# Which side of a trip through HBM is cut into 1 KB rows: the turned blocks of a hybrid SSM and attention encoder layer

## What is computed

```python
h = rms_norm(x, g_mix)
proj = h @ w_in                       # z | xBC | dt_fwd | dt_bwd | q | k | v | gate_ssm | gate_attn
y_ssm = mamba2_bidir(z, xbc, dt_f, dt_b, ...)
y_attn = gqa_bidir_blocks(apply_rope(rms(q)), apply_rope(rms(k)), v)
merged = sigmoid(gate_a) * (y_ssm @ w_ssm_up) + sigmoid(gate_b) * (y_attn @ w_attn_up)
x = x + merged @ w_out
h2 = rms_norm(x, g_mlp)
x = x + square(relu(h2 @ w_mlp_in)) @ w_mlp_out
out = rms_norm(x, g_final)
```

## The kernel before

| rounds | put | get (waits for the put, `s_put`) | first use of what was got (waits `s_got`) |
|---|---|---|---|
| z gate, 4 | p = 6 | p = 1 of the next window | p = 5 |
| rope, 5 | p = 7 | p = 2 of the next window | p = 5 |
| merged, 3, and residual, 3 | p = 1 | p = 3 of the same window | p = 6 |

## Time and profile before

### The profile page before, as it was taken

One profiled execution on the slowest core, in us unless ns is written; L12 is line 12 of the kernel. 1 busy time (PEld: TensorE's weight loads), 2 busy tenths in 40 slices (PEclk: granted clock), 3 DMA queues, 4 the chain that ended last, 5 costly groups with the idle time before them and its releaser, 6 DMA issues.

```text
span 1607.3 us, 20614 instructions
## 1 busy us (share of the span) xinstructions
PE 1595.4 (99%) x7984; PEld 1349.2 (84%) x7984; DVE 1278.8 (80%) x1521; ACT 928.0 (58%) x1264; POOL 79.2 (5%) x67
## 2 busy tenths in 40 slices
PE   9999999999999999999999999999999999999998
PEld 7888888888888888888888888888888888888886
DVE  7978877888767688876666667999899988998893
ACT  7665566665666545554445555665566655655562
POOL 3000000000000134000000000000000000000000
PEclk9999999999999999999999999999999999999999
DMA  7665656665688776545877875558645863686461
GB/s 272 202 201 184 201 183 211 197 198 185 196 244 238 231 225 200 172 145 181 244 265 235 278 228 178 181 171 266 188 133 200 275 192 123 204 281 214 143 244 53
DMA packets 144993, 327.93 MB, mean 204 GB/s; under 512 B 10944, under 2 KB 19328, under 8 KB 144768
## 3 DMA queue, kind: packets, MB, share of 16 engines
q1 hardware_dynamic: 129376, 302.21, 58.5%
q10 hardware_dynamic: 15520, 24.41, 5.2%
HBM read 316.55 MB, written 10.03 MB: 203 GB/s over the span
## 4 chain that ended last, share of the span: by engine, by line
PE 95%; DVE 2%; issue 1%; DMA 1%; ACT 0%; POOL 0%; POOLq 0%; SPq 0%; ACTq 0%
PE G L1835 17%; PE G L1836 17%; PE G L1837 17%; PE G L1844 13%; PE S L1844 7%; PE G L1848 6%; PE S L1835 4%; PE S L1836 4%; PE S L1837 4%; PE S L1848 4%; PE S L1962 1%; DMA raw<-in_w_in 1%; DVE wlo L1108 1%; PE S L1990 0%; PE S L1939 0%
## 5 line engine op out<-in xcount | busy, mean ns | idle before, releaser
L668 ACT ACTIVATE whi<-raw 128x1024 fp32r<-128x1024 f32 x395 | 416.6, 1059 | 396.4 <-PE G L1837 230.4
L1108 DVE TENSOR_TENSOR wlo<-raw,whi 128x1024 fp32r<-128x1024 f32 x395 | 483.3, 1238 | 132.1 <-ACT whi L668 130.5
L1835 PE MATMUL G<-whi,a_both 128*128 128x512 f32 x768 | 300.0, 391 | 2.5 <-DVE wlo L1108 2.0
L1837 PE MATMUL G<-whi,a_both 128*128 128x512 f32 x768 | 299.0, 389 | 0.0
L1836 PE MATMUL G<-wlo,a_both 128*128 128x512 f32 x768 | 299.0, 389 | 0.0
L1844 PE MATMUL G<-a_both,whi 128*128 128x512 f32 x640 | 201.5, 396 | 0.0
L1835 PEld LDWEIGHTS G<-whi,a_both 128*128 128x128 f32 x768 | 144.2, 188 | 34.0 <-issue 2.8
L1837 PEld LDWEIGHTS G<-whi,a_both 128*128 128x128 f32 x768 | 144.2, 188 | 30.2
L1836 PEld LDWEIGHTS G<-wlo,a_both 128*128 128x128 f32 x768 | 144.2, 188 | 28.9
L1848 PEld LDWEIGHTS G<-a_both,wlo 128*128 128x128 f32 x640 | 120.2, 188 | 28.3
L1835 PE MATMUL G<-whi,b_hi 128*128 128x512 f32 x342 | 133.5, 390 | 0.0
(11 more groups left out here) (313 smaller groups left out, 2689.1 us busy)
## 6 DMA issues: line engine op xcount, KB each, us to landing
raw<-in_w_in SPq DMA_DIRECT2D x208, 512.0 KB, 4.4
raw<-in_w_mlp_in SPq DMA_DIRECT2D x74, 512.0 KB, 4.6
raw<-in_w_mlp_out SPq DMA_DIRECT2D x74, 512.0 KB, 4.9
gates<-in_w_mlp_in SPq DMA_DIRECT2D x54, 512.0 KB, 4.2
gates<-in_w_mlp_out SPq DMA_DIRECT2D x54, 512.0 KB, 4.8
raw<-in_w_ssm_up SPq DMA_DIRECT2D x32, 512.0 KB, 3.8
raw<-in_w_attn_up SPq DMA_DIRECT2D x32, 512.0 KB, 4.5
raw<-in_w_out SPq DMA_DIRECT2D x32, 512.0 KB, 5.2
```

The costliest lines, as they stand in the source:

```text
L668: act.activation(high(m), piece(n), ACT.Copy).then_inc(hi_made, 1)
L1108: dve.tensor_tensor(low(m), piece(n), high(m).bitcast(F32), ALU.subtract).then_inc(lo_made, 1)
L1835: pe.matmul(out_ap, hi[:, k, cols], w_hi, start=start, stop=False)
L1837: return pe.matmul(out_ap, lo[:, k, cols], w_hi, start=False, stop=stop)
```

## The change

`put_blocks` issues four transfers instead of one, one for each j. Each takes 128 partitions by 256 floats and writes them as 4 by 32 rows of 1024 bytes, so that the exchange of i and j happens on the way out. `get_blocks` then brings 128 rows of 4096 bytes back with one transfer instead of four. The counts that others wait for follow: `s_put` rises by 64 a round instead of 16, `s_got` by 16 instead of 64. The diff:

```diff
@@ put_blocks
             act.wait_ge(blocks_turned, d + 1)
-            act.dma_start(block_rows[d], src.rearrange("p j c b t -> p (j c b t)")).then_inc(s_put, 16)
+            rows = block_rows[d].rearrange("(j w) (i x) -> j i w x", j=4, i=4)
+            for j in range(4):
+                act.dma_start(rows[j], src[:, j, :, :, :].rearrange("p c b t -> p (c b t)")).then_inc(s_put, 16)
@@ get_blocks
-            act.wait_ge(s_put, 16 * (d + 1))
+            act.wait_ge(s_put, 64 * (d + 1))
             if d:
                 act.wait_ge(lined, d)
-            rows = block_rows[d].rearrange("(i w) (j x) -> j w i x", i=4, j=4)
-            for j in range(4):
-                act.dma_start(dst[Q * j:Q * (j + 1), :, :, :, :].rearrange("w i c b t -> w i (c b t)"), rows[j]
-                              ).then_inc(s_got, 16)
+            act.dma_start(dst[:, :, :, :, :].rearrange("p i c b t -> p (i c b t)"), block_rows[d]).then_inc(s_got, 16)
@@ split_high, and the same in heads_in
-                act.wait_ge(s_got, 64 * (d + 1))
+                act.wait_ge(s_got, 16 * (d + 1))
@@ turn_blocks
-                dve.wait_ge(s_put, 16 * d)
+                dve.wait_ge(s_put, 64 * d)
```

## The result

The changed kernel takes **1641.4 us** (median of 4 runs, 1640.64 to 1644.03) against 1609.44 of the kernel before on the same chip: ratio 1.0197, 95% interval 1.0184 to 1.021. It is 31.7 us slower. The forecast was 1613.4 with a range up to 1626; the sign was right, and the size was eight times too small. The profiled execution took 1640.87 us.

The account below looks back on a forecast made before the run. PE was taken to bound the kernel, busy 99% of the span, so the change could only cost: 1609.39 + 3.5 (third merged round) + 0.5 (five ordinary rounds) = 1613.4 us, range 1608.5 to 1626.

Parts of the forecast that it names:

- the cover of 5.84 us: Steady state of ACT's weight conversions: one may start 5.84 us late before PE runs dry.
- the deadline: Longest time a put may take from issue before PE loses: 12.5 us in the first merged round.
- Four engines: Each put's destination has outermost size 4, so only four DMA engines carry it, 128 rows each; taken with 0.85.
- Two to three of them fall in until ACT stops: 2.5 to 3.7 us: Ordinary merged and residual rounds: weight pieces sharing the put's engines, 1.23 us each, put landing after 10.9 to 12.1 us.
- the prediction's own signs: Main step wrong if small packets stay at 10944; price wrong if PE has gaps in the first two merged rounds.
- My upper bound: Weights alternate packet for packet until four pieces are through: an ordinary put needs 15.1 us, kernel 1626.
- the row with both queues waiting: Profile row: 363 and 362 packets in 3 us, one of each in 132 ns, so engines alternate fairly.
- 0.5 us for all five: Five ordinary merged and residual rounds: ACT stands still some 7 us, PE loses nothing; 0.5 us allowed in all.
- rival 2: All six tight rounds overrun at the wait on `s_put`; 1622 at a put of 14.5 us; chance 0.18.
- The third merged round, 3.5 us for the x loads: Put's remaining 81 rows alternate with x loads and weights; conversion starts at 826.9 against deadline 823.45, costing PE 3.5 us.
- Z and rope rounds nothing: Nine z and rope rounds: puts take 12 to 14.5 us against deadlines of 15 to 16.3, costing nothing.
- The moved issues and the gets: Three issues moved to the put delay ACT by 1.4 us, inside the cover; the single get costs nothing either way.

Follow-up runs that it names:

- experiment 1: Changed kernel with the put's four transfers cut by token group, so the destination's outermost size is 32 and sixteen engines carry it; 1608.99 us, ratio 0.9996.
- 4: Changed kernel with each attn_up piece loading only 64 columns of one row tile, so hardly any weights beside the put; 1631.7 us in one run.
- experiment 5: Kernel with four put transfers over sixteen engines, but the four-engine put in the second merged round alone; 1612.68 us, ratio 1.0018.
- experiment 9: Kernel before the change with a scratch tensor of outermost size 8, one put of 4 KB rows and eight gets; 1628.87 us, ratio 1.0113.
- experiment 7: Kernel with four put transfers over sixteen engines, but four-engine puts in the seven odd rounds; 1621.92 us, ratio 1.0069.
- even and odd rounds: Two kernels with sixteen-engine puts, except four-engine puts in the eight even or the seven odd rounds; 1619.28 us (ratio 1.0052) and 1621.92 us (1.0069).
- experiment 8: Kernel with four put transfers over sixteen engines, but four-engine puts in the three successive merged rounds; 1621.58 us, ratio 1.0073.
- experiment 2: Kernel before the change with a padded scratch tensor of outermost size 4, the put one transfer of 4 KB rows; 1651.92 us, ratio 1.0258.

## Why the prediction was wrong

*What bounds the kernel, and the cover of 5.84 us: right.* No put that landed in time and was followed by one get cost PE anything (experiment 1, and the first two merged rounds of 4), and where one was late PE waited by as much: 2.0 us past the deadline and a gap of 2.31 in the first merged round, 1.4 and 1.7 in experiment 5. What the cover hides is not free for the next round, though (experiment 9).

*Four engines: right.* 720 closing packets fewer, 26.6% of the engines at the end of the put, and the loss gone with sixteen. The Trainium skill's rule ("DMA: Bandwidth & Descriptors", why a DMA increments its semaphore by 16) gave the count for outermost sizes of 4 and, in experiment 9, of 8; this case's packets agree with both.

*"Two to three of them fall in until ACT stops: 2.5 to 3.7 us": wrong, and the step that failed first.* The term was 6.6 us. Four pieces went beside the put, as many as SP's ring has slots, not two to three, and each lengthened it by 1.65 us, not 1.23. I counted the pieces that SP issues while ACT still works, at their average rate. But the four engines carry the put besides their share of weights, so they fall behind the other twelve: whatever weights are queued on them stay there and keep alternating with the put's rows until its last row. The rows' own share was about right (7.04 us and 1.3 around it forecast, 7.9 measured with hardly any weights). By the prediction's own signs it is the price that failed: the small packets fell to 10224, and PE has gaps in the first two merged rounds (2.31 and 4.35 us). My upper bound had the alternation, 15.1 us, beside a measured 14.5; I took the lower end because of the row with both queues waiting, though that row shows just this alternation.

*"0.5 us for all five" ordinary rounds: wrong by the same step.* The puts take 14.4 to 14.6 us in all of them, so rival 2's mechanism, all tight rounds overrun, was the one that came, and at its own 14.5 us it gave 1622.

*The third merged round, 3.5 us for the x loads: wrong as a special case.* Its put takes 14.7 us (827.60 to 842.27), as the others do, not the 15.9 of the forecast. PE's gap there is 3.33 us, close to the 3.5, but that is luck: by itself, in experiment 7, the round makes PE wait 2.79 us, and the rest comes from the late rounds before it.

*Z and rope rounds nothing: nearly right for a round by itself, wrong in a series.* Taken every second one, the nine cost under 2 us together (PE has two waits in the rope rounds, 0.76 and 1.38 us); all at once they cost 7.9, a quarter of the loss. The first z put takes 13.5 us against 16.3 and costs nothing; the fourth, issued late, costs 2.5 us and the clock.

*The sum: wrong in its form.* I added the rounds as if each found ACT and DVE on time. The even and odd rounds together cost 19.5 us, all of them 31.7. The missing 12 us lie in the z, rope and residual rounds above all. What the runs show of their causes is the next put issued late (3.4 us at the fourth z round; 4.0 at the second merged one of experiment 8, behind a backlog of DVE) and PE's granted clock behind its gaps, 8.5 us where the even and odd rounds have 3.4, which had no term. How the rest divides between late puts, late weights and late splits stays open.

*The moved issues and the gets: right.* Four issues take ACT's queue 2.3 us and more where one took 0.34; that is 2.0 more, not 1.4, and it stays inside the cover: the four issues of experiment 1 cost nothing. The single get lands 3.4 us (median) after its issue.

## What to carry to other kernels

Before cutting a transfer differently, read the outermost size of both sides: it decides how many DMA engines carry it, and a transfer on a few engines doesn't take its bytes' time over a few engines, but that plus everything the other queue keeps on those same engines, one packet for one. A deadline holds only for the order that it was read from: with four gets behind the wait instead of one it was 11.1 us and not 12.5. When a wait overruns its cover, do not multiply one overrun by the number of rounds: ask what the late engine does next, whether the next round's start is behind that backlog, and what the clock does after the gap. Before calling a remedy useless, look where the time goes: moving the wait by a piece left the total nearly as it was, yet cured nine rounds of fifteen. If the loss of every second round, taken both ways, doesn't sum to the whole, the rest is compounding.

## What was not expected of the hardware

- One queue on four engines does not get them to itself when the other twelve have next to nothing left: in 786 to 788.8 us the weights' packets on them were 89 beside the put's 113.
- Fewer engines do not make an issue cheaper. One of the changed kernel's took 0.53 us in the median, where the old put of four times the bytes took 0.34 and a quarter of experiment 1's 0.46; the whole put took 0.53 on four engines (experiment 2) and 0.59 on eight (experiment 9).
- Behind PE's longer gaps in the changed kernel and in experiment 8 the granted clock of a few microseconds read 0.57 to 0.74, and matmuls that start 0.23 us apart before the gap start up to 0.43 us apart behind it. In experiment 5, whose gaps are 1.7 and 0.9 us, PE's busy time stayed within 1 us of before (1596.2 us). The length of the gap alone does not tell: behind one of 2.15 us (first merged round, experiment 7) the clock of 786 to 789 us is 0.50, behind one of 2.31 at the same round of the changed kernel that of 792 to 798 us is 1.00.
